# A fused trunk layer on one core: VectorE's and ScalarE's jobs in another order between the projections and in the first output tiles

## The chip, the cores and the metric

The kernel runs on one core of one Trainium2 chip. The metric is the device time of one execution in microseconds, lower is better: the median of repeated runs. A profiled execution has a time of its own, and a span, which is the time from the first to the last recorded instruction.

The engines are called as in the profile: PE is TensorE, DVE VectorE, ACT ScalarE, POOL GpSimd, SP SyncE. They run their own instruction streams and meet at semaphores: an instruction increments a semaphore when it ends, and another engine waits until the count is high enough. All transfers of this kernel are started by SP, one after another in the order of its program, so a transfer whose semaphore is not there yet holds back all transfers behind it.

## What is computed

One layer of a hybrid trunk, cut to what matters here (sequence 1024, width 1024, context 256, four heads):

```python
sh1, sc1, g1, sh2, sc2, g2 = adaln(c, w_mod, b_mod, 6)      # silu(c) @ w_mod + b_mod, six rows of 1024
h = modulate(x, norm1_w, sh1, sc1)
proj = h @ w_in                                             # Q K V, gates, R, conv (CB CC CH), pool (P)
k, v, gates = gla_kvg(...)                                  # gates = log_sigmoid(z @ gate_w + gate_b) / 16
...                                                         # the same for the context's K, V and gates
o_lat, _ = gla_bidir(q, k, v, gates, s_ctx)                 # chunked scan, both directions
y_gla = gla_out(o_lat, r, gla_norm_w)                       # RMSNorm per head, times silu(r)
y_conv, y_pool = short_conv(...), multi_scale_pool(...)
x = x + g1 * (concat(y_gla, y_conv, y_pool) @ w_out)
h2 = modulate(x, norm2_w, sh2, sc2)
x = x + g2 * (square(relu(h2 @ w_mlp1)) @ w_mlp2)
return rmsnorm(x, final_norm_w)
```

## The kernel before

**Tiles.** Features lie on the 128 partitions, tokens along the free axis. A projection tile is 128 output features by 1024 tokens: eight steps k over the input features. Each float32 operand is split into a rounded high part and a low rest (`w_hi`, `w_lo`; `a_hi`, `a_lo`), and each step has three products (high by high, low by high, high by low) for two halves of 512 tokens. PE's results go to two banks of 1024 in `main`, tile by tile in turn; a tile can start only when the tile two before it has been read (`main_free`). The small products (transposes, states, scores, sums of squares) take turns on the two banks of `sm`: job number s waits until job s-2 has been read (`small_free`).

**Weights.** `wstream` holds the weight tiles in order. Tile t is loaded into `raw[t % 2]`, ACT copies its high part (`weight_high`, L1541), DVE subtracts (`weight_low(t)`, L2150) and increments `split_done`; PE waits for `split_done` t+1 ahead of tile t. For the output projection (tiles 20 to 27) POOL makes both parts (L813, L816), except for tile 21.

**The projection stage.** `PROJ` lists 20 tiles: V0 V1 V2 V3 K0 K1 Q0 Q1 P0 P1 CC0 CH0 CB0 R0 R1 CC1 CH1 R2 R3 CB1 (tile 0 to 19). Behind each V tile there is a small gate product g0 to g3, and DVE's `gates(j)` turns it into decayed factors: the minimum of gate and zero, a wait for ACT's logarithm (`gate_log`), a difference, a scan, two differences for the latent part and two for the context (`ku`, `kuc`). Tiles up to K1 also have a context product (L992 to L996), whose last part needs `w_lo`. All other work is planned by hand: `put(tile, k, job)` fills `PLAN`, and every engine goes through the tiles and their steps k and does its part of the jobs that stand at (tile, k). Jobs named here: `A` (scores of a head; on PE L1128, on DVE two masked copies to `a_f`, `a_b` and their sum `a_sum`), `O` (outputs of a head, PE L1150 and L1155; ACT squares them to `sqo` behind the second), `ns` (sums of these squares, PE L1162; ACT turns them into `rso`), `mx` (ACT multiplies the head's 16 states by their decay, L1621, eight instructions a job), `rl` and `rg` (the gate R), `md` (a modulation row).

```python
MIX_AT = (9 * 8, 11 * 8 + 6, 13 * 8 + 2, 14 * 8 + 1)     # slots 8 * tile + k of the jobs "mx"
for _g, _q in enumerate((36, 68)):
    put(_q // 8, _q % 8, "md", _g)
LOW_AT = 3                                               # weight_low(t + 1) at step 3 of tile t
```

**Modulation rows.** `g1` and `sc2` are summed on DVE during the projections: `add_modulation(n)` adds the product of one 128x1024 block of `w_mod` (loaded into `mbuf`) and one column of silu(c) to `macc`; after eight of them PE's job `md` sums over the partitions (L1176), and DVE's `mod_product` (L2233) adds the result to the row. The other two rows are summed in the output stage: `add_late(n)`, n from 0 to 15, adds a block from `mbuf_late` to `macc_late` (L2386). SP loads block n when `late_taken` is n-3, that is when sum n-4 has ended, and its queue has the weight tiles in between: late blocks 6, 7, 8, 9, weight tile 25, late 10 and 11, weight tile 26, late 12 and 13.

**The output stage.** Tiles 20 to 27 multiply the mixed features by `w_out`. Behind each, DVE adds it to the residual (`add(i, b)`, L2402, called X add 0 to 5 below for tiles 20 to 25; it frees the `main` bank), ACT squares the sum, and DVE adds the squares to `acc2` (L2405). The late sums stand between these. Tiles 26 and 27 are done in halves of 512 tokens: the first half of 26, the first half of 27 (which needs X add 5), then the second halves.

**Afterwards** comes the MLP, from 441 us on, as products of Strassen's kind on sums of blocks. It takes some 640 us.

Of the kernel before, what the change touches and what calls it, by code (L numbers as in the profile page):

```python
# [28 lines left out]
HEADS, DK, DV = 4, 64, 128  # L29
# [96 lines left out]
OUT_AT = (10 * 8, 12 * 8, 14 * 8 + 1, 15 * 8 + 4)  # L126
UPD_AT = (0, 0, 11 * 8, 12 * 8 + 6)
CHAIN_AT = (7 * 8 + 1, 8 * 8 + 1, 11 * 8 + 5, 13 * 8 + 2)
MIX_AT = (9 * 8, 11 * 8 + 6, 13 * 8 + 2, 14 * 8 + 1)

BACK_AT = (8, 11, 12, 13)
for _h in range(HEADS):
# [38 lines left out]

LOW_AT = 3

H_ORDER = (4, 5, 6, 7, 0, 1, 2, 3)

# [24 lines left out]
def hybrid_trunk(nc, wstream, wg_in, wm1, wm2, xt, ct, small_in, gw_in, out):  # L202
    ctx = ExitStack()
    with ctx:
# [1875 lines left out]
        def _(dve):  # L2080
# [67 lines left out]
            def weight_low(t):  # L2148
                dve.wait_ge(hi_made, t + 1)
                tt(w_lo[:, t % 2, :, :], raw[:, t % 2, :, :], w_hi[:, t % 2, :, :].bitcast(F32),  # L2150
                   ALU.subtract).then_inc(split_done, 1)
# [88 lines left out]
            def gates(j):  # L2240

                m = M_OF[f"g{j}"]
                dve.wait_ge(tile_done, m + 1)
                ts(t1[:, 0:N], main[:, m % 2, :], one_col("gb", j), 0.0, ALU.add, ALU.min)
                ts(t1[:, N:NA], ob[:, (m % 2) * HALF:(m % 2) * HALF + NC], one_col("gb", j), 0.0, ALU.add,
                   ALU.min).then_inc(gate_min, 1)
                for n in IN_GATES[j]:
                    add_modulation(n)
                dve.wait_ge(gate_min, j + 1)
                dve.wait_ge(gate_log, j + 1)  # L2250
                link(tt(t1[:, :], t1[:, :], t2[:, :], ALU.subtract))
                dve.wait_ge(masks_made, 1)
                link(dve.tensor_tensor_scan(out=t2[:, :], data0=gmask[:, :], data1=t1[:, :], initial=0.0,
                                            op0=ALU.mult, op1=ALU.add))

                f, b = slice(0, DK), slice(DK, P)
                chunks = t2[f, 0:N].rearrange("p (n t) -> p n t", t=CH)
                tt(ku[f, j, :].rearrange("p (n t) -> p n t", t=CH), chunks[:, :, CH - 1:CH].broadcast_to([DK, NCH, CH]),
                   chunks, ALU.subtract)
                ts(kuc[f, j, :], t2[f, N:NA], -1.0, t2[f, NA - 1:NA], ALU.mult, ALU.add)  # L2260
                tt(ku[b, j, :], t2[b, 0:N], t1[b, 0:N], ALU.subtract)
                tt(kuc[b, j, :], t2[b, N:NA], t1[b, N:NA], ALU.subtract).then_inc(gate_dif, 1)
                dve.wait_ge(gate_dif, j + 1)

            def add_modulation(n):

                g, k = n // KT, n % KT
                dve.wait_ge(mbuf_loaded[n % 2], 16 * (n // 2 + 1))
                if k == 0:
                    if g >= 1:  # L2270
                        dve.wait_ge(small_done, S_OF[("md", g - 1)] + 1)
                    ins = ts(macc[:, :], mbuf[:, n % 2, :], silu_c[:, 2 * k:2 * k + 1], None, ALU.mult)
                else:
                    dve.wait_ge(mod_taken, n)
                    ins = stt(out=macc[:, :], in0=mbuf[:, n % 2, :], scalar=silu_c[:, 2 * k:2 * k + 1],
                              in1=macc[:, :], op0=ALU.mult, op1=ALU.add)
                ins.then_inc(mod_taken, 1)
# [75 lines left out]
            after = {"K": after_k, "Q": after_q, "P": after_p, "CH": after_ch, "CB": after_cb}  # L2353
            for t, name in enumerate(PROJ):
                for k in range(KT):
                    if k == LOW_AT and 2 <= t + 1 < NPROJ:
                        weight_low(t + 1)
                    for job in PLAN.get((t, k), ()):
                        if job[0] in jobs:
                            jobs[job[0]](*job[1:])  # L2360
                    if KT * t + k in MOD_SLOT:
                        add_modulation(MOD_SLOT[KT * t + k])
                m, i = M_OF[name], int(name[-1])
                if name == "P0":
                    dve.wait_ge(pads_made, 1)
                if name == "CB1":
                    low_mix(0)
                    low_mix(1)
                if name[:-1] in after:
                    dve.wait_ge(tile_done, m + 1)  # L2370
                    after[name[:-1]](i, m)
                if name[:-1] == "V":
                    gates(i)
# [20 lines left out]
            def residual(m0, g, acc_made, sq_made, nth, before, between):  # L2394

                dve.memset(acc2[:, :], 0.0).then_inc(acc_made, 1)
                dve.wait_ge(acc_made, 1)

                def add(i, b):
                    dve.wait_ge(tile_done, i * 2 + (m0 + b + 1))  # L2400
                    xk = X[:, bass.ds(i * 2 + b, 1), :]
                    stt(out=xk, in0=main[:, 1 - b:2 - b, :], scalar=mods[:, g, bass.ds(i * 2 + b, 1)], in1=xk,  # L2402
                        op0=ALU.mult, op1=ALU.add).then_inc(main_free[1 - b], 1)
                    dve.wait_ge(sq_made, i * 2 + (b + 1))
                    tt(acc2[:, :], acc2[:, :], sq2[:, :], ALU.add).then_inc(acc_made, 1)  # L2405
                    dve.wait_ge(acc_made, i * 2 + (b + 2))

                for i in range(KT // 2 - 1):
                    if i == 2:
                        dve.wait_ge(x2_loaded[1], 16)  # L2410
                    for b in range(2):
                        add(i, b)
                        at = 4 * i + 2 * b + (2 if (i, b) == (0, 0) else 4)
                        for n in range(at, 8 + 4 * i + 2 * b - 2):
                            add_late(n)

                def add_half(k, half, s_out):
                    cols = slice(half * HALF, (half + 1) * HALF)
                    stt(out=X[:, k, cols], in0=main[:, (k + 1) % 2, cols], scalar=mods[:, g, k:k + 1], in1=X[:, k, cols],
                        op0=ALU.mult, op1=ALU.add).then_inc(s_out, 1)  # L2420

                def sum_half(half):
                    cols = slice(half * HALF, (half + 1) * HALF)
                    dve.wait_ge(sq_made, KT - 1 + half)
                    tt(acc2[:, cols], acc2[:, cols], sq2[:, cols], ALU.add).then_inc(acc_made, 1)

                dve.wait_ge(half_done, 2 * nth + 1)
                add_half(KT - 2, 0, res_half)
                sum_half(0)
                dve.wait_ge(half_done, 2 * nth + 2)  # L2430
                add_half(KT - 1, 0, res_half)
                before()
                dve.wait_ge(tile_done, m0 + KT - 1)
                add_half(KT - 2, 1, main_free[1])
                between()
                sum_half(1)
                dve.wait_ge(tile_done, m0 + KT)
                add_half(KT - 1, 1, main_free[0])
# [404 lines left out]
```

## Time and profile before

| | |
|---|---|
| median of 3 runs | 1081.17 us (1080.87 to 1081.6) |
| the profiled execution | 1081.7 us |
| its span | 1079.9 us |
| PE busy | 1055.8 us, 98% of the span |
| DVE busy | 825.2 us, 76% |
| ACT busy | 510.8 us, 47% |
| POOL busy | 307.3 us, 28% |
| mean granted clock of TensorE | 0.997 |
| moved by transfers | 199.82 MB, 185 GB/s |

The profile tells for every instruction when it began and how long it took, and for an idle engine what ended the idle time. The ends of matmuls are modelled, so a PE that waits a little can still seem busy, and the distance from one start to the next says more than the durations. Times of places are microseconds from the start of the span.

### The profile page before, as it was taken

What the parts mean: (1) busy time and instruction counts of PE and PEld (TensorE: products, weight loads), DVE (VectorE), ACT (ScalarE), POOL (GpSimd) and SP (SyncE); (2) the same over time, 40 slices, a digit from 0 to 9 for tenths busy, and PEclk for the clock granted to TensorE, in tenths of its full rate; (3) what the DMA queues carried; (4) which work ended last, traced back from release to release, by engine and by line L of the source; (5) the groups of instructions that cost most, each with busy time, mean ns of one, the idle gap of its engine ahead of it and who ended that gap; (6) DMA issues with size and microseconds to landing.
All of it is one profiled execution on the core that took longest, in us unless ns stands there. A gap on an engine that the chain in (4) does not pass through costs nothing.

```text
span 1079.9 us, 16429 instructions
## 1 busy us (share of the span) xinstructions
PE 1055.8 (98%) x5576; PEld 852.4 (79%) x5576; DVE 825.2 (76%) x1062; ACT 510.8 (47%) x827; POOL 307.3 (28%) x280
## 2 busy tenths in 40 slices
PE   8999999999999999999999999999999999999996
PEld 5678888777778888887888888888778888888884
DVE  4878868647455986899887787877987777787776
ACT  5666533456525222677766666676422222222234
POOL 1000006486101443012332323233322222222323
PEclk9999999999999999999999999999999999999998
DMA  9633331101013664226866666768745844864604
GB/s 352 247 98 118 117 117 40 40 22 40 21 56 120 253 221 169 78 98 234 316 246 260 227 273 233 257 248 298 296 167 234 350 193 178 329 267 179 254 1 156
DMA packets 66646, 199.82 MB, mean 185 GB/s; under 512 B 5664, under 2 KB 15136, under 8 KB 66592
## 3 DMA queue, kind: packets, MB, share of 16 engines
q1 hardware_dynamic: 66592, 199.11, 49.2%
q8 instruction: 33, 0.54, 0.2%
q14 instruction: 21, 0.17, 0.1%
HBM read 139.32 MB, written 59.77 MB: 184 GB/s over the span
## 4 chain that ended last, share of the span: by engine, by line
PE 49%; DVE 5%; issue 1%; DVEq 0%; ACT 0%
PE main L1453 13%; PE ob L1411 13%; PE sm L1411 10%; PE sm L1453 8%; PE ob L1453 6%; DVE stage L2562 1%; DVE XR L2681 1%; DVE XR L2748 1%; DVE slot L2507 1%; DVE slot L2512 1%; DVE stage_last L2562 0%; DVE t_tmp L2555 0%; DVE hid L2569 0%; DVE t_tmp L2546 0%; DVE t_tmp L2541 0%
## 5 line engine op out<-in xcount | busy, mean ns | idle before, releaser
L958 PE MATMUL main<-a_hi,w_hi 128*128 128x512 f32 x376 | 125.9, 416 | 0.0
L1411 PE MATMUL ob<-h_sum,slot 128*128 128x512 f32 x504 | 121.2, 389 | 2.2 <-DVE hid L2569 2.1
L1882 ACT ACTIVATE slot<-raw 128x512 fp32r<-128x512 f32 x80 | 50.2, 631 | 153.1 <-PE main L1453 58.4
L958 PE MATMUL main<-a_lo,w_hi 128*128 128x512 f32 x376 | 116.5, 391 | 0.0
L958 PE MATMUL main<-a_hi,w_lo 128*128 128x512 f32 x376 | 116.2, 390 | 0.0
L1411 PEld LDWEIGHTS ob<-h_sum,slot 128*128 128x128 f32 x504 | 94.5, 188 | 22.5 <-issue 2.5
L2681 DVE SCALAR_TENSOR_TENSOR XR<-main,small,XR 128x512 f32<-128x512 f32 x112 | 83.3, 748 | 28.8 <-PE main L1453 27.7
L958 PEld LDWEIGHTS main<-a_lo,w_hi 128*128 128x128 f32 x376 | 70.6, 188 | 15.6
L958 PEld LDWEIGHTS main<-a_hi,w_lo 128*128 128x128 f32 x376 | 70.6, 188 | 15.5
L958 PEld LDWEIGHTS main<-a_hi,w_hi 128*128 128x128 f32 x376 | 66.7, 188 | 18.0 <-issue 5.8
L1453 PE MATMUL main<-t_even,slot 128*128 128x512 f32 x336 | 78.1, 389 | 0.0
L2507 DVE TENSOR_TENSOR slot<-raw,slot 128x512 fp32r<-128x512 f32 x70 | 62.2, 889 | 17.5 <-ACT slot L1870 17.5
L1411 PE MATMUL sm<-h_hi,slot 128*128 128x512 f32 x224 | 73.6, 390 | 0.2 <-DVE slot L2507 0.2
L1453 PEld LDWEIGHTS main<-t_even,slot 128*128 128x128 f32 x336 | 63.1, 188 | 13.1
L829 POOL TENSOR_TENSOR scaled_state<-tst,decay 64x128 f32<-64x128 f32 x60 | 27.0, 449 | 147.5 <-ACT tst L1614 143.0
L2512 DVE TENSOR_TENSOR slot<-raw,slot 128x512 fp32r<-128x512 f32 x80 | 61.3, 781 | 0.2 <-ACT slot L1882 0.2
L2681 DVE SCALAR_TENSOR_TENSOR XR<-sm,small,XR 128x512 f32<-128x512 f32 x64 | 47.8, 748 | 13.3 <-PE sm L1453 12.4
L919 POOL TENSOR_TENSOR raw<-part_sum,raw 128x512 f32<-128x512 f32 x16 | 21.0, 1313 | 122.2 <-DVE slot L2512 122.2
L890 POOL TENSOR_TENSOR held<-raw 128x512 f32<-128x512 f32 x14 | 23.1, 1653 | 107.7 <-DMA raw<-wstream 59.7
L898 POOL TENSOR_TENSOR held<-raw 128x512 f32<-128x512 f32 x14 | 24.6, 1757 | 90.2 <-DVE slot L2507 90.2
L2681 DVE SCALAR_TENSOR_TENSOR XR<-ob,small,XR 128x512 f32<-128x512 f32 x48 | 35.8, 749 | 18.4 <-PE ob L1453 18.3
L1411 PEld LDWEIGHTS sm<-h_hi,slot 128*128 128x128 f32 x224 | 42.1, 188 | 9.4 <-DVE slot L2507 0.7
(338 smaller groups left out, 2448.3 us busy)
## 6 DMA issues: line engine op xcount, KB each, us to landing
hidden_kept<-stage SPq DMA_DIRECT2D x98, 512.0 KB, 4.3
raw<-wstream SPq DMA_DIRECT2D x60, 512.0 KB, 4.2
t_even<-hidden_kept SPq DMA_DIRECT2D x56, 512.0 KB, 5.4
raw<-wstream SPq DMA_DIRECT2D x16, 1024.0 KB, 5.5
stage<-hidden_kept SPq DMA_DIRECT2D x21, 512.0 KB, 5.1
stage_last<-hidden_kept SPq DMA_DIRECT2D x21, 512.0 KB, 5.9
wmod<-wm SPq DMA_DIRECT2D x8, 1024.0 KB, 10.5
mbuf<-wm SPq DMA_DIRECT2D x16, 512.0 KB, 4.0
```

What stands on the lines that cost most here:

```text
L829: pool.tensor_tensor(scaled_state[DK:P, :], tst[DK:P, h % 2, c, :], decay[DK:P, h, c:c + 1].broadcast_to([DK, DV]), ALU.mult).then_inc(sta ...
L890: pool.tensor_tensor(sums, a21, a22, ALU.add).then_inc(w1_sum, 1)
L898: pool.tensor_tensor(sums, a12, a11, ALU.subtract).then_inc(w1_sum, 1)
L919: pool.tensor_tensor(a11, sums, a11, ALU.subtract).then_inc(w2_sum, 1)
L958: ins = pe.matmul(main[:, bank, half * HALF:(half + 1) * HALF], w[:, slot, k, :], x[:, half * HALF:(half + 1) * HALF], start=begin, stop=end)
L1411: ins = pe.matmul(hid_bank(acc, odd), slots1[j][:, w, kp, :], parts[x][:, kp, :], start=PARTS[j][3] and kp == 0 and m == 0, stop=kp == KP ...
L1453: ins = pe.matmul(product_bank(s, acc, q), slots2[j][:, w, q, kp, :], tset[odd][j][kp][:, x, :], start=begins and kp == 0 and n == 0, stop ...
L1882: act.activation(slots2[j][:, 0, :, :, :], operand(s, j), ACT.Copy).then_inc(w2_hi, 1)
L2507: tt(slots1[j][:, 1, :, :], operand1(b, j), slots1[j][:, 0, :, :].bitcast(F32), ALU.subtract).then_inc(w1_lo, 1)
L2512: tt(slots2[j][:, 1, :, :, :], operand(s, j), slots2[j][:, 0, :, :, :].bitcast(F32), ALU.subtract).then_inc(w2_lo, 1)
L2562: tt(y[:, 1, :], sources(odd)[j], y[:, 0, :].bitcast(F32), ALU.subtract).then_inc(t_lo, 1)
L2681: stt(out=XR[m][:, cols], in0=product_bank(s, acc, q), scalar=mods[:, 3, m:m + 1], in1=XR[m][:, cols], op0=ALU.mult, op1=ALU.add).then_inc ...
```

## The change

Five things move; no instruction is added or taken away.

1. In `gates(0)` DVE's two modulation sums stood between the minimum and the rest. Now they stand at its end, and `weight_low(2)`, which was at step 3 of tile 1, stands ahead of them.
2. `mod_product(0)` on DVE moves from step 4 of tile 4 to the end of `gates(3)`, ahead of `add_modulation(8)` and `weight_low(5)`. PE's part stays.
3. In tile 9 (P1) `weight_low(10)` moves from step 3 to step 4, behind the scores of head 0, first half.
4. ACT's `mx` jobs of head 3 move from steps 1 and 2 of tile 14 (R1) to steps 4 and 5.
5. In the output stage late sum 5 moves from between X add 0 and X add 1 to behind X add 1.

```diff
-MIX_AT = (9 * 8, 11 * 8 + 6, 13 * 8 + 2, 14 * 8 + 1)
+MIX_AT = (9 * 8, 11 * 8 + 6, 13 * 8 + 2, 14 * 8 + 4)
...
-LOW_AT = 3
+LOW_AT = {_t: 4 if _t == 9 else 3 for _t in range(2, NPROJ - 1)}
...
                 ts(t1[:, N:NA], ob[:, (m % 2) * HALF:(m % 2) * HALF + NC], one_col("gb", j), 0.0, ALU.add,
                    ALU.min).then_inc(gate_min, 1)
-                for n in IN_GATES[j]:
-                    add_modulation(n)
+                if j >= 1:
+                    for n in IN_GATES[j]:
+                        add_modulation(n)
                 dve.wait_ge(gate_min, j + 1)
                 dve.wait_ge(gate_log, j + 1)
...
                 tt(kuc[b, j, :], t2[b, N:NA], t1[b, N:NA], ALU.subtract).then_inc(gate_dif, 1)
+                if j == 0:
+                    weight_low(2)
+                    for n in IN_GATES[j]:
+                        add_modulation(n)
+                if j == HEADS - 1:
+                    mod_product(0)
                 dve.wait_ge(gate_dif, j + 1)
...
-                    if k == LOW_AT and 2 <= t + 1 < NPROJ:
+                    if k == LOW_AT.get(t):
                         weight_low(t + 1)
                     for job in PLAN.get((t, k), ()):
-                        if job[0] in jobs:
+                        if job[0] in jobs and job != ("md", 0):
                             jobs[job[0]](*job[1:])
...
                     for b in range(2):
                         add(i, b)
-                        at = 4 * i + 2 * b + (2 if (i, b) == (0, 0) else 4)
-                        for n in range(at, 8 + 4 * i + 2 * b - 2):
+                        first = 4 * i + 2 * b + {(0, 0): 2, (0, 1): 3}.get((i, b), 4)
+                        last = 4 * i + 2 * b + (5 if (i, b) == (0, 0) else 6)
+                        for n in range(first, last):
                             add_late(n)
```

The first place is `gates(0)` on DVE, between tiles 0 and 2: `t_93` and `t_107` are the gate buffers `t1` and `t2`, `macc` the modulation sum, `w_lo` the low part of tile 2's weights. Before:

```order
L2245 TENSOR_SCALAR t_93<-ob,small 128x256
L2272 TENSOR_SCALAR macc<-mbuf,silu_c 128x1024
L2275 SCALAR_TENSOR_TENSOR macc<-mbuf,silu_c,macc 128x1024
L2251 TENSOR_TENSOR t_93<-t_93,t_107 128x1280
L2253 SCALAR_TENSOR_TENSOR t_107<-gmask,t_93 128x1280
L2258 TENSOR_TENSOR ku<-t_107 64x1024
L2260 TENSOR_SCALAR kuc<-t_107 64x256
L2261 TENSOR_TENSOR ku<-t_107,t_93 64x1024
L2262 TENSOR_TENSOR kuc<-t_107,t_93 64x256
L2150 TENSOR_TENSOR w_lo<-raw,w_hi 128x1024
```

And now:

```order
L2245 TENSOR_SCALAR t_93<-ob,small 128x256
L2252 TENSOR_TENSOR t_93<-t_93,t_107 128x1280
L2254 SCALAR_TENSOR_TENSOR t_107<-gmask,t_93 128x1280
L2259 TENSOR_TENSOR ku<-t_107 64x1024
L2261 TENSOR_SCALAR kuc<-t_107 64x256
L2262 TENSOR_TENSOR ku<-t_107,t_93 64x1024
L2263 TENSOR_TENSOR kuc<-t_107,t_93 64x256
L2150 TENSOR_TENSOR w_lo<-raw,w_hi 128x1024
L2279 TENSOR_SCALAR macc<-mbuf,silu_c 128x1024
L2282 SCALAR_TENSOR_TENSOR macc<-mbuf,silu_c,macc 128x1024
```

The two sums over `macc` went behind `w_lo`; everything else kept its order.

The second place is DVE in tile 9: `cpad` and `ypool` are the pooling of tile 8, `w_lo` the weights of tile 10, `a_f`, `a_b` and `a_sum` the scores. Before:

```order
L2305 SCALAR_TENSOR_TENSOR cpad<-pmask,upad 128x1280
L2312 TENSOR_TENSOR ypool<-cpad 64x1024 x2
L2150 TENSOR_TENSOR w_lo<-raw,w_hi 128x1024
L2213 COPY_PREDICATED a_f<-small,sm 128x512
L2213 COPY_PREDICATED a_b<-small,sm 128x512
L2219 TENSOR_TENSOR a_sum<-a_f,a_b 128x512
L2213 COPY_PREDICATED a_f<-small,sm 128x512
```

And now:

```order
L2312 SCALAR_TENSOR_TENSOR cpad<-pmask,upad 128x1280
L2319 TENSOR_TENSOR ypool<-cpad 64x1024 x2
L2213 COPY_PREDICATED a_f<-small,sm 128x512
L2213 COPY_PREDICATED a_b<-small,sm 128x512
L2219 TENSOR_TENSOR a_sum<-a_f,a_b 128x512
L2150 TENSOR_TENSOR w_lo<-raw,w_hi 128x1024
L2213 COPY_PREDICATED a_f<-small,sm 128x512
```

`w_lo` went behind the first `a_sum`, and DVE waits for its own `a_sum` (`a_ready`) before it.

The third place is ACT in tile 14: `tst` are the states of head 3 (job `mx`), `sqo` and `rso` belong to head 2, `rsig` to the gate R0, `w_hi` to the weights of tile 15. Before:

```order
L1541 ACTIVATE w_hi<-raw 128x1024
L1621 ACTIVATE tst<-tst,decay 128x128 x16
L1630 ACTIVATE sqo<-ob 128x1024
L1715 ACTIVATE rsig<-rsig 128x1024
L1489 ACTIVATE rso<-sm,small 128x512
L1495 ACTIVATE rso<-rso 128x512
L1489 ACTIVATE rso<-sm,small 128x512
L1495 ACTIVATE rso<-rso 128x512
```

And now:

```order
L1541 ACTIVATE w_hi<-raw 128x1024
L1630 ACTIVATE sqo<-ob 128x1024
L1715 ACTIVATE rsig<-rsig 128x1024
L1621 ACTIVATE tst<-tst,decay 128x128 x8
L1489 ACTIVATE rso<-sm,small 128x512
L1495 ACTIVATE rso<-rso 128x512
L1621 ACTIVATE tst<-tst,decay 128x128 x8
L1489 ACTIVATE rso<-sm,small 128x512
L1495 ACTIVATE rso<-rso 128x512
```

The sixteen multiplications of the states went behind the squares, in two parts of eight, one ahead of each pair that makes `rso`.

## Rows read from the trace of the kernel before

**Rows 1.** The page, part 1: busy time, share, instructions.

```profile
PE 1055.8 (98%) x5576; PEld 852.4 (79%) x5576; DVE 825.2 (76%) x1062; ACT 510.8 (47%) x827; POOL 307.3 (28%) x280
```

**Rows 2.** Timeline of PE: start, duration, instruction, idle before and its releaser.

```profile
80.36 1.21 PE L996 MATMUL ob<-c_hi,w_lo 128*128 128x256 f32 x8 [0.98 <-DVE w_lo L2150]
...
127.01 0.66 PE L1067 MATMUL sm<-small,vtmp 128*128 128x128 f32 x4 [0.80 <-DVE small L2233]
...
197.59 0.69 PE L1128 MATMUL sm<-qe,ku 64*64 64x64 f32 x32 [0.80 <-DVE a_f L2213]
...
281.60 1.10 PE L1162 MATMUL sm<-sqo,small 128*128 128x512 f32 x2 [1.00 <-ACT sqo L1630]
...
380.16 0.61 PE L958 MATMUL main<-a_hi,w_lo 128*128 128x512 f32 x2
381.18 0.73 PE L958 MATMUL main<-early_hi,w_hi 128*128 128x512 f32 x2 [0.41 <-DVE X L2402]
381.76 0.62 PE L958 MATMUL main<-early_lo,w_hi 128*128 128x512 f32 x2
382.22 0.62 PE L958 MATMUL main<-early_hi,w_lo 128*128 128x512 f32 x2
```

**Rows 3.** Timeline of ACT: the logarithm of gate 0.

```profile
66.52 1.37 ACT L1680 ACTIVATE t<-t,small 128x1280 f32<-128x1280 f32 x1
```

**Rows 4.** Timeline of DVE: gate 0, first and last instruction behind its sums.

```profile
71.61 1.48 DVE L2251 TENSOR_TENSOR t<-t,t 128x1280 f32<-128x1280 f32 x1
...
79.08 1.23 DVE L2150 TENSOR_TENSOR w_lo<-raw,w_hi 128x1024 fp32r<-128x1024 f32 x1
```

**Rows 5.** Timeline of DVE: the modulation row in tile 4.

```profile
126.80 0.16 DVE L2233 TENSOR_TENSOR small<-sm,small 128x8 f32<-128x8 f32 x1
```

**Rows 6.** Timeline of DVE: in tile 9, and beside POOL's states later.

```profile
194.85 1.23 DVE L2150 TENSOR_TENSOR w_lo<-raw,w_hi 128x1024 fp32r<-128x1024 f32 x1
...
197.52 1.35 DVE L2219 TENSOR_TENSOR a_sum<-a_f,a_b 128x512 f32<-128x512 f32 x1
...
274.03 1.31 DVE L2150 TENSOR_TENSOR w_lo<-raw,w_hi 128x1024 fp32r<-128x1024 f32 x1
```

**Rows 7.** Timeline of POOL: in tile 9, and beside the last row above.

```profile
194.90 3.42 POOL L854 TENSOR_TENSOR ypool<-ypool,small 128x1024 f32<-128x1024 f32 x1 [12.20 <-DVE ypool L2312]
198.40 2.37 POOL L855 TENSOR_TENSOR ypool<-ypool,upad 128x1024 f32<-128x1024 f32 x1
...
273.53 0.73 POOL L829 TENSOR_TENSOR scaled_state<-tst,decay 64x128 f32<-64x128 f32 x1
```

**Rows 8.** Timeline of PE: start of tile 10; outputs of head 2; scores of head 3.

```profile
201.07 0.62 PE L958 MATMUL main<-a_hi,w_hi 128*128 128x512 f32 x2
...
276.48 1.15 PE L1155 MATMUL ob<-qe,tst 128*64 128x64 f32 x32
...
287.64 0.69 PE L1128 MATMUL sm<-qe,ku 64*64 64x64 f32 x32
```

**Rows 9.** Timeline of ACT in tile 14: the states, and the second `rso`.

```profile
275.75 4.79 ACT L1621 ACTIVATE tst<-tst,decay 128x128 f32<-128x128 f32 x16 [3.79 <-POOL tst L832]
...
284.99 0.69 ACT L1489 ACTIVATE rso<-sm,small 128x512 f32<-128x512 f32 x1 [0.90 <-PE sm L1162]
```

**Rows 10.** Timeline of DVE in the output stage: late sums and X add 5.

```profile
370.88 9.05 DVE L2386 SCALAR_TENSOR_TENSOR macc_late<-mbuf_late,silu_c,macc_late 128x1024 f32<-128x1024 f32 x4
...
411.44 2.48 DVE L2386 SCALAR_TENSOR_TENSOR macc_late<-mbuf_late,silu_c,macc_late 128x1024 f32<-128x1024 f32 x2
414.16 1.28 DVE L2402 SCALAR_TENSOR_TENSOR X<-main,small,X 128x1024 f32<-128x1024 f32 x1 [0.23 <-PE main L958]
```

**Rows 11.** Timeline of POOL: the split of tiles 25 and 27, first product.

```profile
392.44 2.45 POOL L813 TENSOR_TENSOR w_hi<-raw,small 128x1024 fp32r<-128x1024 f32 x1 [5.83 <-PE main L958]
...
414.20 2.42 POOL L813 TENSOR_TENSOR w_hi<-raw,small 128x1024 fp32r<-128x1024 f32 x1 [4.25 <-PE main L958]
```

**Rows 12.** Transfers, issue to landing: weight tile 25, issued at 380.34.

```profile
raw<-wstream SPq DMA_DIRECT2D x1, 512.0 KB, 6.5
```

## The prediction, made before the change was run

> **What bounds the kernel now.** The first thing to read is the page's busy time: PE is busy for 98% of the span, DVE for 76% [rows 1]. From that a reader takes that a job of another engine costs time only where PE waits for it. The second view is therefore the list of what PE waited for. Up to 440 us, where the change is, it has five entries behind the first 80 us, and each belongs to a place that the change touches; the timeline shows them in brackets [rows 2]: 0.98 for `w_lo` of tile 2, 0.80 for the modulation row in tile 4, 0.80 for the scores' copies in tile 9, 1.00 for head 2's squares in tile 14, 0.41 for X add 1. That is 3.99 us. The third view is the distance between starts, because the ends of matmuls are modelled. Ordinary groups follow each other after 0.46 (381.76 to 382.22). Ahead of the last wait it is 381.18 - 380.16 = 1.02, so 0.56 is lost, and the next group comes after 0.58, 0.12 more than usual: 0.68 in all where the label says 0.41 [rows 2]. I add 0.25 to each other label. If all five went and nothing came in their place, 1.23 + 1.05 + 1.05 + 1.25 + 0.68 = 5.26 us would be gained. That is the upper end.
>
> Does an earlier PE end the kernel earlier? The engines that PE waits for are themselves started by PE (a tile's end, a read bank), so they move with it; the transfers ahead of the output stage are too, and I found no wait of PE for one behind the start. The chain of waits, followed back from the end, is PE's through the MLP but for a few DVE pieces, and DVE's at the MLP's start, where DVE itself was released by PE's last output tile. So I carry a gain through at its full size.
>
> The sum is made against the profiled execution's own time, 1081.7 (span 1079.9); the median of the runs is 0.5 lower, and I take that 0.5 off the result.
>
> **1. gates(0).** ACT's logarithm ends at 66.52 + 1.37 = 67.89 [rows 3], but DVE goes on only at 71.61 [rows 4], because its two sums wait for their blocks' transfers. From there to `w_lo` it is 79.08 - 71.61 = 7.47. Now the gate goes on at about 67.95, `w_lo` begins at 75.4 and ends 1.23 later, at 76.6. PE wants it at 80.36 - 1.23 = 79.1: the wait goes, with 2.5 us to spare. The sums follow on DVE where it would otherwise run into gate 1; the same instructions now hold less waiting, so gate 1 begins no later. What is queued behind: blocks 2 and 3 are loaded once sums 0 and 1 have ended, some 7 us later than before, and gate 1 needs them. A transfer of this size took 6.5 us behind two others [rows 12], less than PE's spare time; if it took 2 more, the wait would move to `w_lo` of tile 3 and cost what it saves. Taken: 1.23, bounds 0 and 1.25.
>
> **2. mod_product(0).** It ran at 126.80 [rows 5], behind one `add_modulation` and one `w_lo`. PE's product for it is long done, so at the end of `gates(3)` it runs two instructions earlier; the `w_lo` alone is 1.2 of that [rows 4], so it runs at 125.6 or before. PE wants the bank at 127.01 - 1.05 = 125.96. `w_lo` of tile 5 comes 0.16 later, and PE reads it only in the last part of a context product. Taken: 1.05; nothing else stands behind the row.
>
> **3. weight_low(10) behind the scores.** This is the edit that I do not take at its face. Before, DVE's `w_lo` began at 194.85 and POOL's product for the pooling at 194.90; POOL's ended at 198.32, 2.24 after `w_lo`'s end at 196.08. DVE's `a_sum` began at 197.52 and took 1.35, ending 0.55 behind POOL's product; POOL's next began at 198.40 and ended 1.90 behind `a_sum` [rows 6, 7]. So these take turns: one waits until the other's instruction is over. The two copies ahead of `a_sum` kept their speed under POOL's product. A later place shows that a waiting POOL gets in even between two DVE instructions: POOL's 273.53 + 0.73 = 274.26, and the `w_lo` that DVE had begun at 274.03 ends 1.08 behind that, at 275.34 [rows 6, 7]. With the new order: copies from 194.85 to 196.35, POOL's first product free of DVE from 194.90 to 197.15, `a_sum` to 197.7, POOL's second product, which waits by then, to 199.6, and only then `w_lo`, to 199.6 + 1.08 = 200.7. PE's scores no longer wait, but tile 10, which began at 201.07 [rows 8] and could now begin at 200.1, waits for `w_lo` until 200.8 or 200.9. Taken: a gain of 0.2. Bounds: 1.05 if DVE's `w_lo` gets in ahead of POOL; -0.3 if POOL's products take 0.5 more. The Trainium skill ("SBUF — State Buffer", Who interferes with whom) says that a VectorE instruction with two SBUF inputs and a GpSimd instruction that reads SBUF exclude each other, and that issue order decides who blocks. The trace agrees (1.35 for an `a_sum` that ends 0.55 behind POOL), and by that rule too POOL's second product, issued first, holds `w_lo` back; without it this term would be 1.05 and the forecast 0.85 lower.
>
> **4. mx of head 3.** The sixteen multiplications ran from 275.75 to 280.54 [rows 9], while the outputs of head 2 had ended at 276.48 + 1.15 = 277.63 [rows 8]. Now the squares begin at 277.7 and are done at 278.7, and PE, which could go on at 281.60 - 1.16 = 280.4, does not wait. Late next is the second `rso` of head 2: ACT does the squares and the exponential (about 1.0 each), eight states (half of 4.79: 2.4), the first pair (0.69 [rows 9] and as much again), eight more states, and then reads the bank from about 285.9 to 286.6; before it was 284.99 to 285.68. PE's scores of head 3 need that bank. They began at 287.64 [rows 8] and now want to at 286.4: a wait of about 0.2. The states are needed by PE only in tile 15. Taken: 1.25 - 0.25 = 1.0; bounds 0.8 and 1.25.
>
> **5. Late sum 5.** Four sums took 9.05 us between the adds, two without POOL beside them 2.48, thus 1.2 each [rows 10]: the rest is DVE waiting for POOL's splits. X add 1 began behind the four sums at 370.88 + 9.05 = 379.9 and ended 1.28 later; without sum 5 it is over by 380.0, and PE wants it at 380.16 + 0.46 = 380.6. Gain 0.68. Behind X add 1 stand three sums instead of two. I followed the turns of DVE and POOL from these durations, a product of POOL at 2.3 and a sum at 1.2; what comes out are estimates. X add 2 ends near 391.3; PE, a tile of 24 groups or 10.9 us later, wants it at 391.5. That is cover of only 0.2. The next thing that is late is on SP's queue: late block 9 waits for sum 5, which ends near 387.7 instead of 379.9 (it stands behind the sum of squares and both products of POOL for tile 24), and weight tile 25 stands right behind it. Its transfer is now issued near 388.2 with two late blocks and tile 26 soon after it. Before, it took 6.5 behind two others [rows 12]; so it lands near 394.7 and POOL's split, which began at 392.44 [rows 11], begins near 394.8. Two products of 2.4 and one turn of DVE later, near 401, it is done; PE wants tile 25 at 402.4. No wait there, and with POOL late DVE gets through two sums alone and X add 3 to 5 are no later. Taken: 0.68.
>
> **Sum.** 1.23 + 1.05 + 0.2 + 1.0 + 0.68 = 4.16 us: 1077.5 for a profiled execution, 1077.0 for the median. What a measurement can tell from no change is about 0.2%, 2.2 us.
>
> **The rivals.**
>
> *The collision with POOL in the output stage.* X add 5 began at 414.16, and POOL's split of tile 27 at 414.20 [rows 10, 11]: DVE was through by 0.04. PE wants X add 5 over by 418.7 (in times of before). In my turns: if tile 25 lands before DVE has summed the third squares (393.6, so within 5.4 us of its issue), POOL's products go first at every turn, X add 4 ends near 411.8, both products of tile 27 come between X add 4 and X add 5, and X add 5 ends near 422.2: a wait of 3.5. Time: 1081.17 - 4.16 + 3.5 = 1080.5, no change that can be measured. For it: 0.04 is little, and the shift is larger. Against it: 5.4 is less than the 6.5 of the row.
>
> *Slower.* The same mechanism at its far end: three products of POOL between X add 4 and X add 5 instead of two, 2.27 more, so a wait of 5.8: 1082.8. It decides from a wait of 4.2 on, that is when X add 5 ends after 422.9. Against it: POOL has only two products for each tile, so the split of tile 26 would have to be late as well.
>
> *Edit 3 at its full size,* `w_lo` ahead of POOL: 0.85 more, 1076.2. Against it is the row at 274.03.
>
> *An edit that does not do what it says.* Blocks 2 and 3 land over 2 us later than the row says and term 1 is lost: 1078.2. Or X add 2, covered by 0.2, is late by 0.5 to 1: 1077.5 to 1078.
>
> **How the numbers follow.** The forecast has 0.56, edit 3 at full size 0.12, a lost term 0.09, the collision 0.18 at 3.5 and 0.05 at its far end. The range goes from 1076.2 (edit 3 at full size) to 1080.7, which takes in the collision at 3.5; the likeliest case's own range is 1076.3 to 1078.0. Faster by over 0.2% means under 1079.0: 0.56 + 0.12 + 0.09 = 0.77. Same: 0.19. Slower: 0.04.
>
> **What would show it.** In the profile of the changed kernel PE's list of waits has no `w_lo` at L996, no modulation row, no `sqo` and no X add 1. New in it are short waits for `w_lo` ahead of tile 10 and for `rso` or the scores' bank in tile 15. `w_lo` of tile 10 lasts about 3 us instead of 1.23, and POOL's first pooling product 2.3 instead of 3.42. In the output stage POOL's split of tile 25 begins some 3 us behind PE's tile boundary, and X add 5 again waits for PE. If X add 5 instead ends more than 5.4 us behind its tile, the forecast is wrong by that wait.

## The result, and the profile after

The changed kernel takes 1083.44 us (median of 10 runs, 1082.42 to 1084.48), the kernel before took 1081.16 beside it (10 runs, 1078.98 to 1081.75): a ratio of 1.0023, 95% interval 1.0015 to 1.0031. It is 2.3 us slower; the forecast was 4.2 us faster. The profiled execution took 1083.6 (span 1081.8, mean granted clock 0.993; before 1079.9 and 0.997).

TensorE's waits above 0.25 in the changed kernel, in the view that groups them (sum in us, how often, the longest):

```profile
PE main L976 <- DVE X L2409: 3.5, 1, 3.5
PE main L1027 <- DMA small<-small_in: 3.1, 1, 3.1
PE ob L1411 <- DVE hid L2577: 2.1, 1, 2.1
PE sm L1453 <- DVE XR L2689: 1.2, 1, 1.2
PE main L1453 <- DVE stage_last L2570: 0.7, 2, 0.5
PE main L1453 <- DVE XR L2689: 0.7, 1, 0.7
PE sm L1020 <- DVE mrow L2158: 0.6, 1, 0.6
PE main L958 <- DVE w_lo L2150: 0.5, 1, 0.5
PE ob L1411 <- DVE slot L2515: 0.3, 1, 0.3
PE main L1035 <- DVE squares L2123: 0.3, 1, 0.3
```

The entries for L996, the modulation row, the scores' copies, `sqo` and X add 1 are gone. On top stands a new one of 3.5 for X, which is X add 5. The other entries of 0.7 and more were there before. Now PE's timeline of the changed kernel (start, duration, instruction, idle before and its releaser) at the places of [rows 2, 8], then at the new wait and at the start of the MLP:

```profile
78.73 1.00 PE L996 MATMUL ob<-c_hi,w_lo 128*128 128x256 f32 x7
...
124.35 0.60 PE L1067 MATMUL sm<-small,vtmp 128*128 128x128 f32 x4
...
194.00 0.69 PE L1128 MATMUL sm<-qe,ku 64*64 64x64 f32 x32
...
198.15 0.73 PE L958 MATMUL main<-a_hi,w_hi 128*128 128x512 f32 x2 [0.51 <-DVE w_lo L2150]
...
233.72 0.69 PE L1150 MATMUL ob<-a_sum,vtok 64*64 64x64 f32 x32 [0.18 <-ACT tst L1621]
...
277.88 1.02 PE L1162 MATMUL sm<-sqo,small 128*128 128x512 f32 x2
...
283.82 0.69 PE L1128 MATMUL sm<-qe,ku 64*64 64x64 f32 x32
...
376.81 0.61 PE L958 MATMUL main<-early_hi,w_hi 128*128 128x512 f32 x2
...
418.62 0.76 PE L976 MATMUL main<-early_hi,w_hi 128*128 128x512 f32 x1 [3.51 <-DVE X L2409]
419.18 0.63 PE L976 MATMUL main<-early_lo,w_hi 128*128 128x512 f32 x1
...
421.97 0.39 PE L976 MATMUL main<-a_hi,w_lo 128*128 128x512 f32 x1
...
506.35 4.57 PE L1411 MATMUL ob<-h_sum,slot 128*128 128x512 f32 x12 [2.06 <-DVE hid L2577]
```

The method for reading this: take one instruction's start in both timelines, subtract, and see where the difference steps. I did that for all matmuls that both traces have. The steps are taken before rounding, so they can differ from the shown leads by 0.01.

| place | start before | after | lead of after | step |
|---|---|---|---|---|
| start of the run | 24.32 | 23.86 | 0.46 | 0.46 |
| `w_lo` of tile 2 (edit 1) | 80.36 | 78.73 | 1.63 | +1.17 |
| modulation row (edit 2) | 127.01 | 124.35 | 2.66 | +1.04 |
| scores, tile 9 (edit 3) | 197.59 | 194.00 | 3.59 | +0.92 |
| tile 10 (edit 3) | 201.07 | 198.15 | 2.92 | -0.67 |
| tile 10, next group | 201.52 | 198.72 | 2.80 | -0.12 |
| outputs of head 1 | 236.26 | 233.72 | 2.54 | -0.26 |
| squares of head 2 (edit 4) | 281.60 | 277.88 | 3.72 | +1.19 |
| tile 23 (edit 5) | 381.18 | 376.81 | 4.37 | +0.65 |
| tile 27, first matmul | 419.39 | 418.62 | 0.77 | -3.60 |
| tile 27, ninth matmul | 421.21 | 421.97 | -0.76 | -1.53 |
| MLP, behind the wait of 2.1 | 505.46 | 506.35 | -0.89 | -0.13 |
| MLP, next group | 508.28 | 510.76 | -2.48 | -1.59 |
| near the end | 1067.33 | 1069.26 | -1.93 | +0.55 |

To tile 23 everything went as forecast: 3.91 us from the edits. Then 3.60 is lost to a wait, and 1.53 more to matmuls that start 0.43 apart instead of 0.23. The view by windows says why (each line: the stretch, its length, PE's busy time and matmuls, its granted clock, DMA share, GB/s):

```profile
410.00:415.00 5.00, 5.00 (x23) 1.00 0.37 142
418.60:421.60 3.00, 2.98 (x7) 0.50 0.83 343
422.00:425.00 3.00, 3.00 (x15) 1.00 0.00 0
507.00:510.40 3.40, 3.40 (x10) 0.51 0.54 222
511.00:514.00 3.00, 3.00 (x15) 1.00 0.96 232
```

TensorE's granted clock is at its lower level, 1.2 GHz, directly behind the wait of 3.51, and again behind the wait of 2.06 at 506.35. The kernel before waits as long at this second place, and its profile shows 1.00 there; its row is

```profile
505.46 2.98 PE L1411 MATMUL ob<-h_sum,slot 128*128 128x512 f32 x12 [2.08 <-DVE hid L2569]
```

The twelve matmuls that take 4.57 above took 2.98. This second stretch costs 1.59 us by the starts of the next group; 0.55 comes back soon after, because the kernel before waits for `slot` at 511.40 and the changed one does not, so 1.0 is lost in all. The Trainium skill ("TensorE: Matmul & The Clock Gate", Part 1: The HAM clock gate) says that an idle TensorE is put to 1.2 GHz and comes back to 2.4 under work. The rows agree: 0.50 behind the waits, 1.00 later. That the wait alone does not decide, they show as well: once with and once without a fall at the same wait.

Who made X add 5 late? VectorE's timeline of the changed kernel:

```profile
388.77 1.22 DVE L2412 TENSOR_TENSOR acc<-acc,sq 128x1024 f32<-128x1024 f32 x1 [1.31 <-ACT sq L1765]
390.03 6.65 DVE L2393 SCALAR_TENSOR_TENSOR macc_late<-mbuf_late,silu_c,macc_late 128x1024 f32<-128x1024 f32 x2
396.61 1.27 DVE L2409 SCALAR_TENSOR_TENSOR X<-main,small,X 128x1024 f32<-128x1024 f32 x1
...
406.82 1.27 DVE L2409 SCALAR_TENSOR_TENSOR X<-main,small,X 128x1024 f32<-128x1024 f32 x1
...
410.65 6.62 DVE L2393 SCALAR_TENSOR_TENSOR macc_late<-mbuf_late,silu_c,macc_late 128x1024 f32<-128x1024 f32 x2
417.20 1.27 DVE L2409 SCALAR_TENSOR_TENSOR X<-main,small,X 128x1024 f32<-128x1024 f32 x1
```

GpSimd's, for tiles 25 and 27:

```profile
389.00 3.28 POOL L813 TENSOR_TENSOR w_hi<-raw,small 128x1024 fp32r<-128x1024 f32 x1 [6.19 <-DMA raw<-wstream]
392.35 3.26 POOL L816 TENSOR_TENSOR w_lo<-raw,w_hi 128x1024 fp32r<-128x1024 f32 x1
...
409.75 3.14 POOL L813 TENSOR_TENSOR w_hi<-raw,small 128x1024 fp32r<-128x1024 f32 x1 [5.13 <-PE main L958]
412.97 3.23 POOL L816 TENSOR_TENSOR w_lo<-raw,w_hi 128x1024 fp32r<-128x1024 f32 x1
```

And the transfer of weight tile 25, issued at 384.30 (issue to landing):

```profile
raw<-wstream SPq DMA_DIRECT2D x1, 512.0 KB, 4.6
```

Tile 25 landed at 388.9, just before VectorE ended its third sum of squares at 389.99. GpSimd's first product was thus waiting, went first (its 3.28 is 1.0 of waiting and 2.3 of work), and so did the second. Sums 8 and 9 took 6.65 instead of 2.48. The same happened at tile 27, where sums 12 and 13 took 6.62 for 2.48 in [rows 10]: both products fall between X add 4 and X add 5.

### The profile page after: what moved, and what is told of

The parts are those of the page before. It is cut to its first block, busy times and chain, and to the rows that moved or that the text cites. A ratio compares the mean times of both kernels' runs of the same rounds, so it can differ in the third digit from the quotient of the medians.

```text
span 1081.8 us, 16431 instructions
## 1 busy us (share of the span) xinstructions
PE 1057.8 (98%) x5576; PEld 854.5 (79%) x5576; DVE 830.6 (77%) x1062; ACT 510.4 (47%) x827; POOL 308.7 (29%) x280
## 4 chain that ended last, share of the span: by engine, by line
PE 50%; DVE 4%; issue 1%; DVEq 0%; ACT 0%
PE ob L1411 13%; PE main L1453 13%; PE sm L1411 10%; PE sm L1453 8%; PE ob L1453 6%; DVE XR L2689 1%; DVE XR L2756 1%; DVE stage L2570 1%; DVE slot L2520 1%; DVE slot L2515 0%; DVE stage_last L2570 0%; DVE t_tmp L2563 0%; DVE hid L2577 0%; DVE t_tmp L2554 0%; DVE t_tmp L2549 0%
```

## The experiments

Each ran beside the kernel before on the same chip. Its median moved between 1080.7 and 1081.4 from one group of runs to the next, so the ratios are the thing to compare. The experiments' diffs are against the changed kernel unless another is named.

**no_edit5.** The bounds of the loop over the late sums as they were.

```diff
-                        first = 4 * i + 2 * b + {(0, 0): 2, (0, 1): 3}.get((i, b), 4)
-                        last = 4 * i + 2 * b + (5 if (i, b) == (0, 0) else 6)
-                        for n in range(first, last):
+                        at = 4 * i + 2 * b + (2 if (i, b) == (0, 0) else 4)
+                        for n in range(at, 8 + 4 * i + 2 * b - 2):
```

> The changed kernel without edit 5 (late sum 5 back ahead of X add 1). Theory T (edit 5 alone makes the 3.5 us wait for X add 5, and that wait makes TensorE's granted clock fall to 0.50 behind it): no wait for X add 5, granted clock 1.00 around 418 to 422, X add 1's 0.65 lost again, the gains of edits 1 to 4 kept (1.17 + 1.04 - 0.13 + 1.19 = 3.27 us by the starts of TensorE's instructions): 1077.9 us. Rival R (the second fall of the clock, at 506, has nothing to do with the wait at 415): it stays and costs its 1.2 to 1.4: 1079.2. Rival E (edits 1 to 4 by themselves shift TensorE against the transfers, so X add 5 is late without edit 5 as well): 1081 or more.

Measured: 1078.66, ratio 0.9979 (0.9970 to 0.9987). The wait for X add 5 is gone, X add 1 waits 0.41 again. Edits 1 to 4 are a gain, and adding edit 5 turns it into a loss. The clock fell at the start of the MLP all the same, as rival R had it for that place. The wait there was 3.10, not 2.08.

**only_edit5.** The kernel before with edit 5's part of the diff and nothing else.

> The kernel before with edit 5 alone. Theory T: X add 1 gains 0.65, X add 5 waits about 3.5, the clock falls behind it (1.5): 1081.16 - 0.65 + 3.6 + 1.5 = 1085.6 us, 1086.8 if the second fall at the start of the MLP comes too. Rival E (the wait needs the earlier edits' shift): 1080.5. The record's forecast for edit 5: 1080.5 too (0.68 faster).

Measured: 1085.96, ratio 1.0045 (1.0032 to 1.0058). PE waits 3.51 for X add 5, and the following matmuls are slow for longer than in the changed kernel: 2.7 is lost behind the wait instead of 1.5. Edit 5 makes the wait without any help from the others. At the start of the MLP PE then waits 3.03, and there the clock does not fall (one row of the timeline, and one window with a granted clock of 1.00 throughout):

```profile
509.89 2.98 PE L1411 MATMUL ob<-h_sum,slot 128*128 128x512 f32 x12 [3.03 <-DVE hid L2570]
```

```profile
498.00:515.00 17.00, 13.97 (x63) 1.00 0.62 247
```

So the 1085.96 is near theory T's 1085.6 by a somewhat different sum.

**filled_wait.** Work for PE in place of idleness.

```diff
                 for b in range(2):
+                    if fill and b == 1:
+                        for k in range(fill):
+                            pe.matmul(main[:, 1, HALF:N], w_hi[:, 0, k % KT, :], parts(k % KT)[0][:, HALF:N], start=True, stop=True)
                     pe.wait_ge(split_done, t_ready + b)
...
+            last_pair(KT // 2 - 1 + (M_OUT - 2) // 2 + 1, T_OUT + KT - 1, acc2_made, 0, sums2_done, mix_parts, MIX_ORDER, fill=14)
```

> The changed kernel with 14 extra matmuls of 512 columns (3.2 us at 0.227 each) ahead of TensorE's wait for X add 5, written to the half bank that tile 26 fills later from its start; their results are used by nothing. Theory T (the clock falls because TensorE stood idle): the labelled wait shrinks from 3.5 to about 0.3, tile 27 begins when it did, granted clock 1.00 from 418 to 422: 1083.44 - 1.5 = 1081.9 us; 1080.6 if the fall at 506 goes as well. Rival (the fall at 418 is only where it is in time and does not follow from idleness): the clock falls all the same, 1083.4.

Measured: 1081.19, ratio 0.9999 (0.9990 to 1.0009). PE's timeline has a wait of 0.37 and the usual distance behind it:

```profile
417.97 0.47 PE L976 MATMUL main<-early_hi,w_hi 128*128 128x512 f32 x1 [0.37 <-DVE X L2412]
418.27 0.40 PE L976 MATMUL main<-early_lo,w_hi 128*128 128x512 f32 x1
418.50 0.39 PE L976 MATMUL main<-early_hi,w_lo 128*128 128x512 f32 x1
```

X add 5 is as late as before (3.60 lost at this point, as in the changed kernel), yet the time is 0.0024 of 1081, or 2.6 us, lower. 1.5 of it is the clock at 418. The rest is not shown by a trace; it would fit the MLP's start if the clock falls there in only a part of the runs (their mean clocks are 0.995 to 0.997, those of the changed kernel 0.993 to 0.996). In the profiled execution it did fall there, behind a wait of 2.08.

**block10_first.** Only the landing of tile 25 is moved.

```diff
-            for i in range(6, 10):
+            for i in range(6, 11):
                 load_late(i)
...
-                for i in range(2 * (t - T_OUT), min(2 * (t - T_OUT) + 2, NLATE)):
+                for i in range(2 * (t - T_OUT) + (t == T_OUT + 5), min(2 * (t - T_OUT) + 2, NLATE)):
                     load_late(i)
```

> The changed kernel with one transfer moved on SyncE's queue: late block 10, which waits for late sum 6, goes ahead of weight tile 25, so tile 25 is issued about 1.2 us later (385.5 instead of 384.3) and lands near 390.5 instead of 388.9. Everything else, edit 5 too, stays. Theory T in its full form (the wait comes because tile 25 lands before VectorE's third sum of squares at 388.8 to 390.0, so GpSimd's products go first at every turn from there on): now VectorE's sum of squares and late sum 8 begin ahead of GpSimd's first product, X add 5 is on time, no fall of the clock at 418: 1083.44 - 3.6 - 1.5 = 1078.3 us, 1077.1 without the second fall. Rival Q (three late sums behind X add 1 are too many wherever the transfer lands): the wait of 3.5 stays, 1083.4.

Measured: 1078.06, ratio 0.9970 (0.9958 to 0.9981). Tile 25 was issued at 385.02, 0.7 later, and took 6.0 instead of 4.6. VectorE's timeline from the third sum of squares on:

```profile
388.32 1.23 DVE L2412 TENSOR_TENSOR acc<-acc,sq 128x1024 f32<-128x1024 f32 x1 [1.31 <-ACT sq L1765]
389.58 2.48 DVE L2393 SCALAR_TENSOR_TENSOR macc_late<-mbuf_late,silu_c,macc_late 128x1024 f32<-128x1024 f32 x2
391.98 1.28 DVE L2409 SCALAR_TENSOR_TENSOR X<-main,small,X 128x1024 f32<-128x1024 f32 x1
...
409.21 1.28 DVE L2409 SCALAR_TENSOR_TENSOR X<-main,small,X 128x1024 f32<-128x1024 f32 x1 [0.41 <-PE main L958]
```

GpSimd's first product for tile 25:

```profile
391.19 3.13 POOL L813 TENSOR_TENSOR w_hi<-raw,small 128x1024 fp32r<-128x1024 f32 x1 [8.85 <-DMA raw<-wstream]
```

A transfer that lands 2.2 us later makes X add 5 begin 8 us earlier (409.21 for 417.20), and now it waits for PE. In this execution PE was 0.5 further ahead from the start on; seen from PE, the transfer lands 2.7 later and X add 5 begins 7.5 earlier. Rival Q falls.

**tile25_early.** The opposite: tile 25 ahead of late block 9 (`range(6, 9)` and `- (t == T_OUT + 5)`).

> The changed kernel with weight tile 25 ahead of late block 9 on SyncE's queue (the opposite of block10_first): tile 25 lands some 4 us earlier, before TensorE frees its place, so GpSimd's product begins at TensorE's tile boundary near 388.0. Theory T (who comes first at the third sum of squares decides): GpSimd is first again, a wait for X add 5 of about 3.1 by my turns, and the clock falls behind it: 1083.0 us. Rival L (tile 25 comes too late behind late block 9 and that lateness makes the wait): no wait, 1078.3.

Measured: 1083.06 in the one run, PE waits 3.08 for X add 5, and the clock falls behind it. Rival L falls, as far as one run can tell: it is not lateness that hurts but who comes first. GpSimd began at 387.66, ahead of the sum of squares at 388.50, which then took 2.66.

**sum13_later.** Sum 13 moves behind X add 5.

```diff
-                        last = 4 * i + 2 * b + (5 if (i, b) == (0, 0) else 6)
+                        first -= (i, b) == (2, 1)
+                        last = 4 * i + 2 * b + (5 if (i, b) in ((0, 0), (2, 0)) else 6)
```

> The changed kernel with late sum 13 moved from ahead of X add 5 to behind it. Theory T: X add 5 then has one sum and one product of GpSimd less ahead of it; by my turns it ends 0.2 us late at most: wait 0 to 0.4, no fall of the clock near 418: 1083.44 - 3.4 - 1.5 = 1078.5 us. Rival (the late engine is something else, a transfer or ScalarE's squares): the wait stays over 2.

Measured: 1080.00, ratio 0.9983 (0.9973 to 0.9992). X add 5 was over at 414.51, about when PE wanted it, but my 0 to 0.4 was wrong, and so was 1078.5. PE waited for another engine:

```profile
415.61 0.50 PE L976 MATMUL main<-early_hi,w_hi 128*128 128x512 f32 x1 [1.16 <-POOL w_lo L816]
```

GpSimd's split of tile 27 ended at 412.31 + 3.24 = 415.55. It was no earlier in the changed kernel: there it ended at 412.97 + 3.23 = 416.20, also after PE wanted the tile (418.62 - 3.60 = 415.02), and was hidden behind X add 5, which ended at 418.47. The collision has two sides, and my turns watched only VectorE's. At the start of the MLP this profile lost 2.9 to the fallen clock, behind a wait of 3.14, which is a part of what is missing. The rival falls: no wait over 2 was left at this place.

**mlp_filled.** block10_first with 12 matmuls ahead of the wait at the start of the MLP.

```diff
+                    parts = h_set(j)
+                    if j == 6 and nth == 1:
+                        for n in range(12):
+                            pe.matmul(main[:, 0, 0:HALF], slots1[j][:, 0, n % KP, :], parts[0][:, n % KP, :], start=True, stop=True)
                     if j == 6:
                         pe.wait_ge(y_added, i * 3 - 4)
-                    parts = h_set(j)
```

> block10_first with 12 extra matmuls of 512 columns (2.7 us) ahead of the wait of 3.0 at 498 to 501, to a bank that nothing uses then; their results are used by nothing. Theory T (idle time of TensorE brings the fall of the clock at 502): wait 0.3, no stretch at 0.50 near 502, the next group begins when it did: 1078.06 - 1.4 = 1076.7 us. Rival (the fall there does not follow from idleness): 1078.1.

Measured: 1077.19, ratio 0.9958 (0.9945 to 0.9972), the fastest of all. By windows (block10_first had a mean of 0.52 from 502 to 505.5):

```profile
498.00:501.90 3.90, 3.51 (x16) 1.00 0.24 99
502.00:505.50 3.50, 3.50 (x16) 1.00 0.87 357
```

The gain over block10_first is 1.3 us by the ratios, whose intervals overlap, so the size is not settled. The profiles show the mechanism: PE's lead over the kernel before goes from 4.15 ahead of this stretch to 4.03 behind it, in block10_first from 4.94 to 3.35.

**before_mlp_filled.** The kernel before with 8 such matmuls.

> The kernel before with 8 extra matmuls of 512 columns (1.8 us) ahead of its wait of 2.08 at 503.4 to 505.5, to a bank that nothing uses then; their results are used by nothing. Its runs so far lie between 1079 and 1084 with mean granted clocks of 0.998 down to 0.993. Theory T (in a part of its runs the clock falls behind that wait, which costs 1.4 or 2.9): with the wait filled no run has a mean clock of 0.995 or less, the runs lie within 1.5 us of each other, and the median falls by 0.3 to 1.2 us. Rival (the spread has another cause): clocks and spread stay as they are.

Measured: 1080.74, ratio 0.9998 (0.9989 to 1.0007). All eleven runs have clocks of 0.996 to 0.998, so that part of the theory holds. The runs still spread over 2.7 us and the median did not move: the clock is not the only thing that varies.

**no_edit3.** block10_first with `weight_low(10)` at step 3 again (`LOW_AT` 3 for all tiles).

> block10_first without edit 3. By the starts of TensorE's instructions: the wait of 0.80 for the scores' copies is back (0.92 lost), the wait of 0.51 for w_lo ahead of tile 10 is gone (0.68 won), so edit 3 is worth 0.25 as the record forecast; if the short wait for head 1's states at 233 to 236 (0.38) also comes from edit 3, it is gone, and edit 3 is worth -0.1; if it comes from the other edits it stays. Time 1078.1 to 1078.5.

Measured: 1078.25 in the one run. The wait of 0.81 for the scores is back, the one ahead of tile 10 is gone. At head 1's outputs 0.25 is still lost. This wait (label 0.18) stands in 6 of the 12 profiles, in before_mlp_filled too, which has none of the edits, and not in block10_first, which has edit 3; so it comes and goes between executions and is not edit 3's. From 127 to 281.6 PE's lead grows by 0.97 without edit 3 and by 1.05 in the changed kernel, both with this wait: edit 3 is worth 0.1. In block10_first, without it, the lead grows by 1.28.

**no_edit1.** block10_first with the two sums and `weight_low(2)` where they were.

> block10_first without edit 1. Two profiles of the old order of gates(0) (only_edit5, before_mlp_filled) showed waits for w_lo in tile 2 of 0.64 and 0, where the kernel before had 0.98, since VectorE's first modulation sum began at 67.33 and 66.97 instead of 69.16. Theory V (edit 1 removes a wait whose size depends on when that block's transfer lands, and so differs from run to run): the wait in this profile is between 0 and 1, and the median is 0.3 to 1.0 us above block10_first's ratio of 0.9970, so a ratio of 0.9973 to 0.9980. Rival (1.2 us in every run, as the record's forecast has it): ratio 0.9981 or more.

Measured: 1078.50, ratio 0.9980 (0.9971 to 0.9989). VectorE's first sum began early, as in the other two profiles of the old order:

```profile
67.31 0.75 DVE L2274 TENSOR_SCALAR macc<-mbuf,silu_c 128x1024 f32<-128x1024 f32 x1 [4.58 <-DMA mbuf<-wm]
```

PE had no wait for `w_lo` in tile 2. Four profiles of the old order thus show 0.98, 0.64, 0 and 0. The ratio lies 1.1 us above block10_first's with overlapping intervals, at the edge between theory and rival, so the median worth of edit 1 stays open between 0 and 1.2.

## Why the prediction was wrong

**Terms 1 to 4 held.** Forecast 1.23, 1.05, 0.2 and 1.0; by the starts of this pair of profiles 1.17, 1.04, 0.13 (0.92 - 0.67 - 0.12) and 1.19. Of term 1, no_edit1 shows that 1.2 is the size of this pair and not of every run. Term 3 came by its own steps: `w_lo` of tile 10 took 2.93, GpSimd's first pooling product 2.41, PE waited 0.51 ahead of tile 10. What I did not have was the 0.26 at the outputs of head 1, which belongs to no term. In term 4 the wait of 0.2 for the second `rso` did not come: it was read at 282.91, and the scores began at 283.82.

**Term 5 is the step that failed**, and in it one number. X add 1 gave its 0.65. Late sum 5 ended near 383.9 (late block 9, which waits for it, was issued at 383.91), which with PE's lead of 4.37 is 388.3 in times of before, near the 387.7 that I had. Then the prediction said: "Before, it took 6.5 behind two others [rows 12]; so it lands near 394.7". It took 4.6, and landed at 388.9, ahead of the end of the third sum of squares at 389.99. I had worked out that 5.4 was the point from which the collision decides, and took one row of another place in the queue for the price of a transfer. In block10_first, where late blocks 9 and 10 stood ahead of it, the same tile took 6.0; in the changed kernel, with one block just ahead, 4.6. The profiles together bear this out: 4.4 to 4.6 in the four with block 9 alone just ahead, 6.0 to 6.4 in the four with block 10 there too, and 6.0 to 6.9 in the three with late sum 5 in its old place. The row was right for its own place. One row with 1.1 of margin was not worth odds of three to one.

**The rival "collision with POOL in the output stage" is what happened**, with its size: wait 3.5 forecast, 3.51 measured, both products of tile 27 between X add 4 and X add 5. That the size is met to 0.1 is in part luck: in times of before X add 5 ended at 422.8 instead of 422.2, and PE wanted it at 419.2 instead of 418.7; the errors of 0.6 and 0.5 all but cancel. block10_first (landing 2.2 later, no wait) and tile25_early (landing earlier, 3.08) show that the order of the turns at the third sum of squares decides. The Trainium skill ("SBUF — State Buffer", Who interferes with whom) says that issue order decides who blocks, and the trace agrees: at 389.00 GpSimd waits ahead of the late sum, in block10_first at 389.58 the late sum is first.

**No case of mine held the clock.** With the wait of 3.5 I had 1080.5; the kernel took 1083.44. The wait costs 1.5 more behind it, because TensorE stood idle: filled_wait keeps X add 5 just as late and runs at 1.00 there. Another 1.0 is lost at the start of the MLP; by the starts these two and some 0.5 in small pieces (0.1 from the edits, 0.2 at the wait, 0.15 for `slot` at 498.56) make up the distance. There the clock falls in the profile of the changed kernel and not in that of the kernel before. From the mean clocks (0.993 to 0.998 in the kernel before, 0.993 to 0.996 in the changed one) I take that it falls there in a part of the runs of the one and in nearly all of the other; no trace of those runs shows the place.

"I carry a gain through at its full size" holds only as long as the clock does. In block10_first the lead goes from 4.94 to 3.35 across this stretch, with the wait filled (mlp_filled) only from 4.15 to 4.03. That is why block10_first stands at 0.9970, some 1077.9, and not at 1077.0. VectorE, which is back to back there (10.00 busy of 10 us), also reached this point 0.5 later relative to PE in the profiles of no_edit5 and block10_first, so that PE waited 3.0 to 3.1 instead of 2.08; but these 0.5 came back a group later, where PE no longer waited for `slot`. Why the clock falls behind one wait of about 2.1, or of about 3.0, and not behind another of the same length stays open.

## What to carry to other kernels

Where VectorE and GpSimd take turns, ask who is waiting first at the first turn: here a transfer that landed 2.2 us earlier moved the far end by 8 and made a wait of 3.5, and the order is cheap to choose (one transfer moved on the queue gave 5.7 us here, 1.0023 to 0.9970). Take a transfer's time from a row with the same neighbours in the queue (4.4 to 6.9 us for one and the same tile here); if the margin to a known cliff is smaller than the spread of such rows, the cliff is the forecast or gets half of the chance. A wait of two or three microseconds on a busy TensorE can have a second price in the granted clock behind it. In the twelve profiles 11 of 13 waits of over 2 us had it, 1.4 to 1.7 us each, and 2.7 and 2.9 where it lasted longest; waits of 1.2 had none. Add it to such a stall in a sum with a chance of its own, and where the wait can't be removed, try matmuls into a free bank in its place: that took the fall away at X add 5 (filled_wait) and at the start of the MLP (mlp_filled), though in the kernel before it did not move the median.

## What was not expected of the hardware

- Waits of TensorE of 2.06 to 3.51 us in a stream that is otherwise busy were followed, 11 times in the twelve profiles, by a stretch at a granted clock of 0.50 (distance of 512-column matmuls 0.43 instead of 0.23); a wait of 2.08 in the kernel before and one of 3.03 in only_edit5 were not.
- The same kernel shows different mean clocks from run to run, 0.993 to 0.998 for the kernel before, and with its wait at the start of the MLP filled 0.996 to 0.998.
- VectorE's first modulation sum began between 66.97 and 69.16 in four profiles with the same order there, since it waits for a transfer.
